# Four weight tiles multiplied before the inverse root is known, at five norms

## The reference, cut to what matters

```python
def rms_norm(x, g):                     # one per token
    return x * lax.rsqrt(jnp.mean(x * x, axis=-1, keepdims=True) + EPS) * g
def modulate(h, shift, scale):
    return h * (1 + scale) + shift
# block 1
x = x + peer_ffn(rms_norm(x, ffn_norm), w_q, ...)          # product "pq": norm 5
# block 2, layer 0, then layer 1
h = modulate(rmsnorm(x, mix_norm_g[0]), shift0, scale0)    # products "eq", "ef", "ek", "ev": norm 6
x = x + gate * merge(diff_attention(h))
h = modulate(rmsnorm(x, ffn_norm_g[0]), ...)               # swiglu: (silu(h@w1) * (h@w3)) @ w2: norm 8
h = modulate(rmsnorm(x, mix_norm_g[1]), ...)               # conformer_conv, products "pw1": norm 9
h = modulate(rmsnorm(x, ffn_norm_g[1]), ...)               # swiglu again: norm 11
```

## Time and profile before

| | us |
|---|---|
| median of 3 runs | 1994.74 (1993.57 to 1997.96) |
| the profiled execution | 1994.48 |
| its span | 1992.7 |
| PE busy | 1820.2 (91%) |
| DVE, ACT, POOL busy | 940.0, 873.8, 856.7 |
| mean granted TensorE clock | 0.965 of full |

### The profile page before, as it was taken

One profiled execution on the slowest core, in us unless ns is written; L12 is line 12 of the kernel. 1 busy time (PEld: TensorE's weight loads), 2 busy tenths in 40 slices (PEclk: granted clock), 3 DMA queues, 4 the chain that ended last, 5 costly groups with the idle time before them and its releaser, 6 DMA issues.

```text
span 1992.7 us, 37237 instructions
## 1 busy us (share of the span) xinstructions
PE 1820.2 (91%) x13992; PEld 1664.1 (84%) x13992; DVE 940.0 (47%) x1569; ACT 873.8 (44%) x1315; POOL 856.7 (43%) x432
## 2 busy tenths in 40 slices
PE   6998899999999988999999978996799978879997
PEld 5886798999999877788888877964699978569997
DVE  2564239650000477566666634245444456634444
ACT  4354254555555455454554542133244444324443
POOL 3400369897888899000000044200355546015552
PEclk8999899999999999999999988988899989989999
DMA  5363454554555578655555541100355533035553
GB/s 201 96 241 125 142 171 159 177 168 158 179 182 185 197 262 261 203 191 194 194 191 195 194 156 64 64 11 9 117 181 180 187 130 127 22 106 182 181 186 106
DMA packets 85340, 312.67 MB, mean 157 GB/s; under 512 B 9601, under 2 KB 9601, under 8 KB 84865
## 3 DMA queue, kind: packets, MB, share of 16 engines
q1 hardware_dynamic: 84960, 309.41, 46.8%
q0 software_dynamic: 288, 1.97, 0.3%
HBM read 310.29 MB, written 1.05 MB: 156 GB/s over the span
## 4 chain that ended last, share of the span: by engine, by line
PE 82%; POOL 7%; DVE 5%; issue 3%; ACT 2%; DMA 1%; DVEq 0%; SPq 0%; POOLq 0%; ACTq 0%
PE psr L670 42%; PE acc L917 18%; PE acc L670 6%; PE psr L659 5%; POOL sq L2008 4%; POOL wl L484 3%; PE psr L897 2%; PE acc L730 1%; PE psr L646 1%; PE psr L1062 1%; DVE rinv L1528 1%; ACT wh L475 1%; DVE sq L1547 1%; PE psr L985 1%; PE psr L766 1%
## 5 line engine op out<-in xcount | busy, mean ns | idle before, releaser
L484 POOL TENSOR_TENSOR wl<-ring,wh 128x1024 fp32r<-128x1024 f32 x286 | 710.9, 2489 | 617.8 <-ACT wh L475 617.4
L475 ACT ACTIVATE wh<-ring 128x1024 fp32r<-128x1024 f32 x458 | 482.4, 1055 | 558.9 <-PE psr L670 497.4
L670 PE MATMUL psr<-hh,wh 128*128 128x256 f32 x2200 | 554.3, 288 | 63.6 <-DVE hl L1561 60.8
L670 PE MATMUL psr<-hl,wh 128*128 128x256 f32 x2200 | 550.8, 287 | 0.0
L670 PEld LDWEIGHTS psr<-hh,wh 128*128 128x128 f32 x2200 | 431.7, 196 | 69.0 <-issue 65.1
L670 PEld LDWEIGHTS psr<-hl,wh 128*128 128x128 f32 x2200 | 431.8, 196 | 0.5 <-issue 0.2
L670 PE MATMUL psr<-hh,wl 128*128 128x256 f32 x2200 | 311.9, 285 | 9.7 <-POOL wl L484 9.7
L484 DVE TENSOR_TENSOR wl<-ring,wh 128x1024 fp32r<-128x1024 f32 x172 | 213.1, 1239 | 176.7 <-ACT wh L475 176.7
L670 PEld LDWEIGHTS psr<-hh,wl 128*128 128x128 f32 x2200 | 286.0, 193 | 11.9 <-POOL wl L484 11.9
L2013 POOL DMA_DIRECT2D arena<-in_consts x1 | 0.8, 757 | 360.0 <-DVE x L1810 360.0
L917 PE MATMUL acc<-wh,hh 128*128 128x512 f32 x512 | 137.2, 390 | 1.5 <-ACT wh L475 1.5
(11 more groups left out here) (269 smaller groups left out, 2407.0 us busy)
## 6 DMA issues: line engine op xcount, KB each, us to landing
ring<-in_peer_u SPq DMA_DIRECT2D x128, 512.0 KB, 3.2
ring<-in_peer_v SPq DMA_DIRECT2D x128, 512.0 KB, 3.2
ring<-in_ada_w SPq DMA_DIRECT2D x96, 512.0 KB, 4.4
ring<-in_ffn_a SPq DMA_DIRECT2D x44, 512.0 KB, 3.9
ring<-in_ffn_b SPq DMA_DIRECT2D x44, 512.0 KB, 3.3
ring<-in_ffn_d SPq DMA_DIRECT2D x44, 512.0 KB, 3.3
ring<-in_pw SPq DMA_DIRECT2D x24, 512.0 KB, 3.3
ring<-in_w_in SPq DMA_DIRECT2D x18, 512.0 KB, 3.7
```

The source lines that it names most:

```text
L475: nc.scalar.activation(wh[:, q % 2, :], ring[:, s, :], ACT.Copy).then_inc(high_ready, 1)
L484: eng.tensor_tensor(wl[:, q % 2, :], ring[:, n % NS, :], wh[:, q % 2, :], ALU.subtract)\
L670: return mm(out, w, a, start=start, stop=stop, skip_group_check=True)
```

## The change

At norms 5, 6, 8, 9 and 11 the first four weight tiles no longer wait for `h`. ACT multiplies `x` by the norm's gain alone (`raw_h`, two instructions a piece, right behind the piece's square), DVE makes the low part of that (`raw_l`), and `raw_product` multiplies them with the tile; in the first of the four the matmuls of the sum are laid between the pieces. At the four modulated norms two more columns stand behind the 256 tokens in `raw_h`, the high and the low part of the shift, so the same matmul gives shift @ w. Afterwards DVE multiplies the result by `rinv` and adds the shift's column (`raw_shift`, and for silu and the sigmoid as ACT's bias). `h` is still made, for the fifth and later tiles: by `normalise` (L1623 and L1631 or L1634 of the changed kernel) in one pass without the shift, which ACT adds with `hh` and DVE with `hl`. The first norm too is made by `normalise`, whose pieces of `h` and `hl` alternate.

```diff
-    g += [("norm", 6)] + [("q", c) for c in range(3)] + [("f", 0), ("norm", 7)]
+    g += [("norm", 6), ("q", 2), ("f", 0), ("norm", 7)]
+            def raw_product(n, out, width, start=True, sums=None, turn=0):
+                b = split_no(n) % 2
+                ...
+                pe.wait_ge(high_ready, split_no(n) + 1)
+                for k in range(KC):
+                    if sums is not None and k % 2 == 0:
+                        pe.wait_ge(squares, squares_before(sums) + k // 2 + 1)
+                        for c in (k, k + 1):
+                            last = mm(ps[:, 0:T], ones, sq[:, c * T:(c + 1) * T], ...)
+                        ...
+                        pe.wait_ge(raw_low, 4 * turn + k // 2 + 1)
+                    w = wh[:, b, k * P:(k + 1) * P]
+                    mm(out[:, 0:width], w, raw_h[:, k, 0:width], ...)
+                    mm(out[:, 0:T], w, raw_l[:, k, :], ...)
+                low_ready(pe, n)
+                for k in range(KC):
+                    last = mm(out[:, 0:cols], wl[:, b, k * P:(k + 1) * P], raw_h[:, k, 0:cols], ...)
+                last.then_inc(tile_used, 1)
@@ ACT: norm
+                if first is not None:
+                    split_high(first)
+                if shift is not None:
+                    A(raw_h[:, :, T:T + 1], shift.unsqueeze(2), ACT.Copy).then_inc(shift_high, 1)
                 ...
                     A(sq[:, c0 * T:c1 * T], src[:, c0:c1, :], ACT.Square).then_inc(squares, 1)
+                    if gain is not None:
+                        for c in (c0, c0 + 1):
+                            ins = A(raw_h[:, c, 0:T], src[:, c, :], ACT.Copy, scale=gain[:, c:c + 1])
+                        ins.then_inc(raw_high, 1)
+                    if first is not None and q == 1:
+                        split_high(first + 1)
@@ ACT: behind the root (norms 6 and 9; 5 likewise)
-            first_highs("eq", 0)
             rootof(6)
-            h_highs(6, 2)
+            highs_after(("eq", 0))
+            h_highs(2, mod(0, 0), (0, 1))
+            highs_after(("eq", 1))
+            h_highs(2, mod(0, 0), (2, 3))
@@ DVE
+            def normalise(turn, gain, shift=None):
+                def piece(q):
+                    for c in (2 * q, 2 * q + 1):
+                        ins = STT(out=h[:, c, :], in0=x[:, c, :], scalar=gain[:, c:c + 1], in1=rinv[:, :],
+                                  op0=ALU.mult, op1=ALU.mult)
+                    ins.then_inc(h_made, 1)
+                def low(q):
+                    dve.wait_ge(h_high, 4 * turn + q + 1)
+                    ...
+                            ins = STT(out=hl[:, c, :], in0=h[:, c, :], scalar=shift[:, c:c + 1], in1=hh[:, c, :],
+                                      op0=ALU.add, op1=ALU.subtract)
+                    ins.then_inc(h_low, 1)
+                piece(0)
+                for q in range(4):
+                    if q < 3:
+                        piece(q + 1)
+                    low(q)
+            def raw_lows(turn, gain, q):
+                dve.wait_ge(raw_high, 4 * turn + q + 1)
+                for c in (2 * q, 2 * q + 1):
+                    ins = STT(out=raw_l[:, c, :], in0=x[:, c, :], scalar=gain[:, c:c + 1], in1=raw_h[:, c, 0:T],
+                              op0=ALU.mult, op1=ALU.subtract)
+                ins.then_inc(raw_low, 1)
+            def shift_low(turn, shift):
+                dve.wait_ge(shift_high, turn)
+                TT(raw_h[:, :, T + 1:T + 2], shift.unsqueeze(2), raw_h[:, :, T:T + 1], ALU.subtract)
@@ DVE: ffn, steps 0 and 1
+                    if f < 2 and it is None:
+                        rescale_a(f)
+                        if f == 0:
+                            normalise((3, 5)[layer], gsc[:, (2, 4)[layer], :], mod(layer, 3))
+                        used(dve, TILE_NO["b", layer, f])
+                        raw_shift(small[:, 10 + f:11 + f], psr[bb])
+                        drains(TT(fg[:, f, :], psr[bb][:, 0:T], rinv[:, :], ALU.mult), ("fb", layer, f))
+                        dve.wait_ge(silued_raw, 2 * layer + f + 1)
+                        STT(out=fg[:, f, :], in0=fg[:, f, :], scalar=small[:, 10 + f:11 + f], in1=fs[:, f, :], ...)
```

More of the change, by code:

```diff
@@ L172, in plan_groups @@
     g.append(("norm", 9))
-    g += [(what, c) for what, c in conv_order() if what != "rep"]
+    g += [(what, c) for what, c in conv_order() if what != "rep" and (what, c) not in (("pw1", 0), ("pw1", 1))]
     g += [("norm", 10)] + [("pw2", c) for c in range(4)]
@@ L1074, in _ @@
             for what, c in conv_order():
[L1075 to L1076 removed]
+                if what == "pw1" and c < 2:
+                    for m in range(2):
+                        raw_product(TILE_NO["pw1", 2 * c + m], acc[2 * c + m], T + 2, sums=9 if c == m == 0 else None, turn=3)
+                elif what == "pw1":
+                    split_features("pw1", c, [(("pw1", c), h_parts)], turn=4 if c == 2 else None)
                 elif what == "rep":
@@ L1099, in _, with norm @@
             A = nc.scalar.activation
-            def norm(k, src, n, waits, prev=None, piece_ready=None):
+            def norm(k, src, n, waits, prev=None, piece_ready=None, gain=None, shift=None, first=None):
                 for s, v in waits:
@@ L1678, in _ @@
                 drains(TT(xs, ps[:, :].rearrange("p (c t) -> p c t", c=2), xs, ALU.add), ("wo", c))
+                drained(dve, ("wo", c))
+                if c:
+                    raw_lows(0, par("ffn_norm"), c - 1)
+            raw_lows(0, par("ffn_norm"), 3)
             norm(5)
-            apply(x, h, par("ffn_norm"), KC, normed)
-            h_lows(1)
+            normalise(1, par("ffn_norm"))
+            for c in range(2):
+                ps = full(dve, ("pq", c))
+                drains(TT(qT[:, 2 * c:2 * c + 2, :], ps[:, :].rearrange("p (c t) -> p c t", c=2),
+                          rinv[:, :].unsqueeze(1).broadcast_to([P, 2, T]), ALU.mult), ("pq", c))
             def top16(vals, idx, rows):
@@ L1810, in _ @@
                 drains(TT(xs, ps[:, :].rearrange("p (c t) -> p c t", c=2), xs, ALU.add), ("vt", q))
+                drained(dve, ("vt", q))
+                if q:
+                    raw_lows(1, gsc[:, 1, :], q - 1)
+            raw_lows(1, gsc[:, 1, :], 3)
             norm(6)
-            peer_added(dve)
-            modulate(x, h, gsc[:, 1, :], mod(0, 0), normed)
-            h_lows(2)
+            normalise(2, gsc[:, 1, :], mod(0, 0))
+            for m in range(4):
+                used(dve, TILE_NO["eq", m])
+                raw_shift(small[:, 8 + m:9 + m], acc[m])
+                st.do(TT(qf[:, m, :], acc[m][:, 0:T], rinv[:, :], ALU.mult))
+                st.do(TS(qf[:, m, :], qf[:, m, :], small[:, 8 + m:9 + m], None, ALU.add))
             norm(7)
@@ L1909, in gate @@
             def gate(c):
+                if c < 2:
+                    used(dve, TILE_NO["pw1", 2 * c + 1])
+                    for m in range(2):
+                        n = 2 * m + c
+                        raw_shift(small[:, 8 + n:9 + n], acc[2 * c + m], pb[:, 2 * c + m:2 * c + m + 1])
+                    TT(csig[:, c, :], acc[2 * c + 1][:, 0:T], rinv[:, :], ALU.mult).then_inc(rescaled, 1)
+                    up = upad[:, c, PADL:PADL + T]
+                    st.do(TT(up, acc[2 * c][:, 0:T], rinv[:, :], ALU.mult))
+                    dve.wait_ge(gates, c + 1)
+                    STT(out=up, in0=up, scalar=small[:, 8 + c:9 + c], in1=csig[:, c, :], op0=ALU.add, op1=ALU.mult)\
+                        .then_inc(gated_raw, 1)
+                    return
                 ps = full(dve, ("pw1", c))
@@ L1970, in _ @@
                 drains(ins, ("pw2", c))
-            for c in range(4):
                 drained(dve, ("pw2", c))
```

228 lines of the change are left out of this document (149 added, 79 removed).

## The result

The changed kernel takes 2001.59 us (median of 20 runs, 1994.11 to 2004.69); the kernel before, run beside it as often, takes 1996.70 (1991.80 to 2000.39). The ratio is 1.0023, 95% interval 1.0012 to 1.0034: slower by 0.23%, some 4.6 us. Forecast were 1997.5 us against 1994.74, a ratio of 1.0014. The profiled execution after took 1998.60 us, its span is 1996.8; against the 1992.7 of before that is 4.1 more.

The account below looks back on a forecast made before the run. PE bounds the kernel, standing still 50.60 us at five norms, waiting for DVE; 1994.48 - 0.4 (gain at full clock) + 3.2 (half clock) = 1997.3, as median 1997.5 us. Own range 1991 to 2004, with rivals 1980 to 2006.

Parts of the forecast that it names:

- The term that eats it: DVE instructions with two SBUF inputs are blocked by POOL's splits, each losing up to 2.4 us.
- the walk: Queue-by-queue timing of the changed kernel at each norm, with PE at 2.4 GHz throughout: 0.4 us gained in all.
- Norm 11, queue by queue: At norm 11 the hole moves to other places: rinv 1785.2, normalise until 1796.7, d0 1799.5 to 1802.3; 2.1 us lost.
- The other norms: Norm 5 gains 2.2 us, norm 6 loses 0.5, norm 8 loses 1.4, norm 9 gains 1.2, norm 0 gains 1.0.
- Norm 0's forecast of 1.0: Norm 0 gains 1.0 us, bounds 0 and 2, as hl's first piece no longer waits for eight instructions of h.
- The clock: PE's first tiles at the five norms may run at 1.2 GHz: 0 to 6.4 us together, half taken, 3.2.
- The sum at full clock: Gains and losses of all norms with PE at 2.4 GHz throughout: 0.4 us gained.
- The blocking hardly binds: Rival: no DVE instruction is ever blocked at the norms, 38.3 us gained with norm 0, 1956 us; chance 8%.
- It binds half the time: Rival: DVE's instructions come in runs while POOL waits, half of 38 us gained, 1977 us; chance 16%.
- The slower rival: Half clock through four early tiles at every norm, d0's hole a full 5 us at norms 8 and 11: 2006; 19%.
- Signs named ahead: Profile signs: raw_l maxima 2.5 to 2.8 us, PE waits at tiles four and five, d0 holes 4 to 6, later rinv.
- the signs against it: normalise done within 8 us of rinv; PE idle under 20 us at the five norms in sum; granted clock 0.99.

Follow-up runs that it names:

- e1: Changed kernel with POOL filling zeros in place of the early tiles' low parts, which are missing from the result: 0.9842 of the kernel before.
- e3: Changed kernel without early products at any norm, keeping only the new one-pass making of h: 0.9991 of the kernel before.
- e4: Changed kernel with early products only at norms 5 and 9, h in one pass at norms 6, 8 and 11: 0.9976 of the kernel before.
- e5: Changed kernel, POOL's padding and diagonals behind the first splits (norm 8), ACT's shift copy before the first high part (norm 11): 0.9989 of the kernel before.
- e6: Changed kernel with the first gate ahead of normalise at norms 8 and 11, and d0's parts moved into normalise: 1.0017 of the kernel before.
- e8: Changed kernel with the edits of e5 and e6 together: 0.9990 of the kernel before.

## Why the prediction was right, step by step

- **The term that eats it** was the blocking of DVE by POOL's splits: the mechanism was right. Shown, by e1: without it the same program is 36 us faster, and without it the kernel before only 5. Predicted medians near 0.47 us with maxima of 2.5 to 2.8 came as 0.480 and 5.1; the mean of 0.9 came as 0.72. For `sq<-x,gsc,rinv` the maximum is 2.6 and the mean 0.77. The maximum of `raw_l` was too low: the walk had two instructions meet two splits at norm 6, and it was one that sat through both, to nearly the same end.
- **Norm 11, queue by queue.** `shift_low` caught from 1767.46 to 1769.8 (the walk had 1766.8 to 1769.1), `rinv` ready at 1785.6 (1785.2), `normalise` done at 1797.0 (1796.7), d0 from 1800.0 (1799.5). The walk missed only that d0 would run at half clock, to 1805.3 and not 1802.3: 3.6 lost for the 2.1 forecast.
- **The other norms.** Norm 9: 0.7 gained for 1.2 forecast, though e3 and e4 show that the one pass gains it. Norm 6: 2.2 lost for 0.5; the clock takes 1.6 in the first tile and 1.7 in the fifth. Norm 8: 2.0 lost for 1.4; free of the 2.8 and 2.4 us that the clock takes there it would have gained 3. The walk's 1447.5 for d0 fits its loss of 1.4 only as the end of d0. In the times of the kernel before (the stage's cut is 2.46 us earlier after) d0 ended at 1449.4, and the fourth tile at 1438.6 for the walk's 1439.3, though it had the 2.8 of half clock in it. Norm 5: 4.7 gained for 2.2, of which e3 puts 2.4 down to the one pass. There the walk ran 1.2 us late from `normalise` on (begun at 227.3 for 228.5, fourth tile ended at 236.6 for 237.9), and the half clock took 1.7 of that back: the fifth tile ended at 242.3 for 242.9, 3.1 us ahead of the kernel before. The other 1.6 of the stage's 4.7 comes later, where the same code moves by 1. Norm 0's forecast of 1.0 cannot be told from 187.1 against 187.1 where the same code moves by 7.
- **The clock** was the mis-sized term. The sum at full clock said 0.4 gained. The profile, with the 9.2 us of the first four stretches at 1.2 GHz taken out and norm 10 left aside, says 4.7 - 0.6 + 3.2 + 0.7 - 1.2 = 6.8; with the 6.0 of the fifth tiles too, 12.8, if all of it counts. The clock was put at 3.2, half way to a bound of 6.4, and cost 9.2 to 15.2, so even the bound was too low. I had looked for it in the first tiles. At norms 5 and 9 the first tiles ran at full clock (1.00 granted from 216 to 232 and from 1628 to 1645); at norms 6, 8 and 11 it fell in the new holes, most of all before d0, and at norms 5, 6 and 9 before the fifth tile. The two errors, 6.4 to 12.4 on the one side and 6.0 to 12.0 on the other, have nearly cancelled, and norm 10's 1.7, which is not shown to be the change's, adds to the second. That the total was met within 2 us is in that part luck.
- **The rivals.** "The blocking hardly binds" fell with e1. "It binds half the time" would have given 1977: fallen. The slower rival, half clock through all four early tiles at every norm, is not what happened (the clock was back within the second tile). Its hole before d0 came (5.5 and 4.7 for a full 5), and its clock term of 6.4 was nearer than the forecast's 3.2, but its total of 2006 was too high: the ratio of 1.0023 is 1999.3 in the terms of 1994.74.
- **Signs named ahead.** A hole of 4 to 6 us before the first `acc<-fgh` at norms 8 and 11: 5.49 and 4.68. `rinv` later by 3 to 8 at the modulated norms: 7.4, 3.4, 2.9 and 7.1 us, each counted from the stage's cut (absolute, 7.6 at norm 11). Waits for the fourth and fifth tile's `wh`: 1.3 and 4.35 at norm 9. None of the signs against it came: PE waited 24.0 us at norms 8 and 11 alone, at norm 11 `normalise` was done 11.4 us after `rinv`, and the granted clock was 0.968.

## What to carry to other kernels

When a change moves DVE instructions with two SBUF inputs to where POOL reads SBUF, ask what POOL does then before asking how long they take: an instruction of 0.48 us took 2.5 to 5.1, and one of 8 columns 2.3. Moving the instructions that block to the engine that they block beat every reordering tried here (e5, e6, e8), even though it adds to the engine that PE waits for: 1.23 us on DVE in place of 2.35 on POOL turned a loss of 0.2% into a gain of 1.0%. And several short holes were not cheaper here than a long one: behind each of 4.3 to 5.5 us PE came back at half clock, and twice behind one of under 2 us.
